# A hybrid backbone step on one core: a third expert fixed ahead of the router, three sets of weight homes, the first expert's rows by selection products

## What is computed

```python
def trunk_layer(P, l, x, cond, ...):
    mod = jnp.dot(jax.nn.silu(cond), P["w_ada"][l]) + P["b_ada"][l]
    sh1, sc1, g1, sh2, sc2, g2 = jnp.split(mod[:, None, :], N_MOD, axis=-1)
    h = rmsnorm(x, P["norm1"][l]) * (1 + sc1) + sh1
    ... four mixers ...
    x = x + g1 * jnp.einsum("blm,md->bld", mixed, P["w_out"][l])
    h = rmsnorm(x, P["norm2"][l]) * (1 + sc2) + sh2
    x = x + g2 * moe_ffn(h, P["w_router"], ...)

def moe_ffn(x, w_router, router_bias, w_gate, w_up, w_down):
    probs = softmax(t @ w_router)           # 384 x 16
    ... best of 4 groups, top 2 inside it, weights normalised ...
    h = silu(t @ w_gate[e]) * (t @ w_up[e]) # 1024 -> 512
    h = h * gates[..., None]
    return sum over e of h @ w_down[e]      # 512 -> 1024
```

## Time and profile before

| | |
|---|---|
| median of 3 runs | 661.88 us |
| profiled execution | 664.11 us, span 662.3 us |
| PE, DVE, ACT, POOL busy in the span | 85%, 37%, 21%, 10% |
| mean granted clock of PE | 0.945 |
| bytes moved | 176.16 MB, 266 GB/s over the span |
| 16 loads each of gate, up and down weights | 2048 KB each |

### The profile page before, as it was taken

The page is one execution under the profiler, slowest core; times in us unless marked ns, Lnnn a source line. Parts: engine busy times, 40 slices in busy tenths (PEclk is TensorE's granted clock), DMA queues, the critical chain, the costliest instruction groups (busy, mean ns, idle before and its releaser), DMA issues.

```text
span 662.3 us, 13154 instructions
## 1 busy us (share of the span) xinstructions
PE 563.9 (85%) x5670; PEld 367.7 (56%) x5670; DVE 246.3 (37%) x526; ACT 137.8 (21%) x260; POOL 66.2 (10%) x98
## 2 busy tenths in 40 slices
PE   2789999999999899599964899999777777867974
PEld 0575544566675566574443799997344444434531
DVE  2551648887736824720358611011000000001025
ACT  1330562422128601010141111000000000000012
POOL 1039000000003100020002000000000000300031
PEclk9989999999999999899977699999999999979988
DMA  8989830303110914961597599999999999999972
GB/s 265 392 300 368 308 128 0 128 1 127 55 74 10 374 72 153 356 176 63 190 406 279 187 353 387 398 384 389 393 396 395 395 396 396 394 365 412 405 273 100
DMA packets 79277, 176.16 MB, mean 266 GB/s; under 512 B 6072, under 2 KB 11199, under 8 KB 78847
## 3 DMA queue, kind: packets, MB, share of 16 engines
q1 hardware_dynamic: 64848, 149.01, 60.6%
q0 software_dynamic: 6032, 18.75, 8.3%
q10 hardware_dynamic: 8351, 7.73, 3.5%
HBM read 163.01 MB, written 12.47 MB: 265 GB/s over the span
## 4 chain that ended last, share of the span: by engine, by line
PE 23%; SPq 19%; DMA 8%; issue 4%; DVE 2%; ACT 1%; POOL 1%; ACTq 0%; DVEq 0%; POOLq 0%
SPq L1091 17%; PE psum L874 6%; PE psum L799 5%; PE psum L871 4%; DMA slot<-in_w_down 3%; PE psum L882 2%; PE psum L806 2%; SPq L1105 2%; DMA y_rows<-ye 1%; DMA h_rows<-ye 1%; DMA slot<-y_rows,rows 1%; DMA xe<-h_rows,lst 1%; PE psum L813 1%; POOL slot L1244 1%; PE psum L459 1%
## 5 line engine op out<-in xcount | busy, mean ns | idle before, releaser
L882 PE MATMUL psum<-slot,xeTa 128*32 128x256 f32 x1536 | 98.9, 415 | 28.8 <-DMA slot<-in_w_gate 25.3
L547 PE MATMUL psum<-hT,slot 128*128 128x384 f32 x304 | 100.8, 489 | 0.0
L882 PEld LDWEIGHTS psum<-slot,xeTa 128*32 128x32 f32 x1536 | 57.4, 119 | 69.7 <-issue 28.8
L547 PEld LDWEIGHTS psum<-hT,slot 128*128 128x128 f32 x304 | 56.9, 190 | 38.2
L882 PE MATMUL psum<-slot,heT 128*32 128x256 f32 x768 | 45.3, 389 | 6.3 <-DMA slot<-in_w_down 6.3
L871 PE MATMUL psum<-slot,xeTa 128*32 128x384 f32 x384 | 44.8, 509 | 0.5 <-ACT xeTa L1542 0.5
L874 PE MATMUL psum<-slot,xeTa 128*32 128x128 f32 x384 | 45.3, 282 | 0.0
L874 PEld LDWEIGHTS psum<-slot,xeTa 128*32 128x32 f32 x384 | 43.4, 114 | 0.6
L556 PE MATMUL psum<-slot,hT 128*128 128x512 f32 x96 | 42.3, 596 | 1.1 <-DMA slot<-in_w_in 1.1
L2214 DVE COPY heT<-psum 128x256 f32<-128x256 f32 (+1 forms) x16 | 7.3, 457 | 95.8 <-PE psum L902 95.8
L1550 ACT ACTIVATE he<-psum 128x256 f32<-128x256 f32 (+1 forms) x16 | 6.6, 410 | 154.9 <-PE psum L882 126.9
(11 more groups left out here) (429 smaller groups left out, 774.8 us busy)
## 6 DMA issues: line engine op xcount, KB each, us to landing
slot<-in_w_gate SPq DMA_DIRECT2D x16, 2048.0 KB, 23.2
slot<-in_w_up SPq DMA_DIRECT2D x16, 2048.0 KB, 18.8
slot<-in_w_down SPq DMA_DIRECT2D x16, 2048.0 KB, 19.7
slot<-in_w_ada SPq DMA_DIRECT2D x12, 2048.0 KB, 15.4
slot<-in_w_in SPq DMA_DIRECT2D x7, 2048.0 KB, 9.0
y_rows<-T POOLq DMA_DIRECT2D x11, 384.0 KB, 15.4
slot<-in_w_out SPq DMA_DIRECT2D x2, 2048.0 KB, 16.3
y_rows<-ye ACTq DMA_DIRECT2D x22, 128.0 KB, 6.8
```

The costliest lines, as they stand in the source:

```text
L547: last = mm(o[:, 0:TOK], w[:, kt, tile(i)], hT[:, kt, :], start=(kt == 0), stop=(kt == KT - 1))
L882: last = mm(psum[32 * c:32 * c + 32, bank, 0:HALF], x(k, c % 2), w(k)[:, c // 2 * HALF:c // 2 * HALF + HALF], start=(k == 0), stop=(k == t ...
```

## The change

1. **A third fixed expert.** `order` puts experts 0, 1 and 2 first. Expert 2's blocks have homes of their own, made of pieces: seven eighths of its gate block lie over constants that only the mixers need, the rest over the new GX, over G1 (the gate of the first residual), hT, badar (the modulation bias) and SELW, which lies over the selection matrices SEL. A load of such a set is 2 + 3 + 5 DMAs. Each piece of expert 2 goes out when what lies there has been used.
2. **Three sets in rotation.** Experts 0 to 11 take the sets n % 3, the last four n % 2. A load waits for the last user of its set, that is n - 3. The loops over ten experts are written out.
3. **Expert 0's rows by products.** DVE writes the 0/1 matrix ONE, PE multiplies it with `h2tok` and gets the rows already turned (24 products, 96 columns each), and ACT copies them to `xeT`. No gather, no turning. `lst2` holds expert 1's list alone and stands between the two halves of these products. The second and third part of the later lists are now made inside the first gate product.
4. **Block 11** of the modulation, on PE, moves from behind `lst2` to before the wait for the router's result. Its sum on DVE (`modrow_out(11)`) moves forward too.
5. **G2** no longer has a tile of its own. It lies over the down home of set 0, and POOL loads it when expert 14's down product is done; G2P is issued behind it.

```diff
-    put("order", np.tile((15 - np.arange(16) + np.array([20000, 10000] + 14 * [0]))[None], (P, 1)))
+    put("order", np.tile((15 - np.arange(16) + np.array([30000, 20000, 10000] + 13 * [0]))[None], (P, 1)))
...
-        G2 = eb("G2", [P, 2, D])
+        GX = eb("GX", [P, 4, CW])
+        G2 = slot[home(0, 2)][:, 0:4, :].rearrange("p (c k) n -> p c (k n)", c=2)
...
+        hTf = hT[:, :, :].rearrange("p k n -> p (k n)")
+        g1f = G1[:, :, :].rearrange("p c n -> p (c n)")
+        spent = cols["dft_ctx"][0]
+        assert cols["mask_b"][0] + P - spent >= (KT - 1) * CW
+        third_gate = [const[:, spent + k * CW:spent + k * CW + CW] for k in range(KT - 1)] + [GX[:, 0, :]]
+        third_up = [GX[:, k, :] for k in range(1, 4)] + [g1f[:, k * CW:k * CW + CW] for k in range(4)] + \
+                   [hTf[:, 2 * CW:3 * CW]]
+        badarf = badar[:, :, :].rearrange("p n g -> p (n g)")
+
+        def of_set(n):
+            return n % 3 if n < 12 else n % 2
+
+        def use(n):
+            return sum(of_set(m) == of_set(n) for m in range(n))
+
+        def user_before(n):
+            return max(m for m in range(n) if of_set(m) == of_set(n))
+        SEL1 = hTf[:, 0:NT * P].rearrange("p (j n) -> p j n", j=NT)
+        ONE = hTf[:, CW:CW + NT * ROWS].rearrange("p (j n) -> p j n", j=NT)
...
+        SELW = eb("SELW", [P, D])
+        third_down = [[hTf[:, 3 * CW:4 * CW], hTf[:, 4 * CW:5 * CW]], [badarf[:, 0:CW], badarf[:, CW:2 * CW]],
+                      [SELW[:, 0:CW], SELW[:, CW:2 * CW]], [hTf[:, 5 * CW:6 * CW], badarf[:, 2 * CW:3 * CW]]]
...
+            ada(11)
             pe.wait_ge(s["route"], 1)
             o = claim(pe, "places")
             for j in range(NT):
...
-            o = claim(pe, "lst2")
+            for j in range(NT):
+                for half in range(2):
+                    taken(pe, ("h2", j, half))
             pe.wait_ge(s["sel"], 1)
-            for e in range(2):
-                for j in range(NT):
-                    last = mm(o[:, e:e + 1], SEL[:, 2 * j + e, :], tokid16[:, j:j + 1], start=(e == 0 and j == 0),
-                              stop=(j == NT - 1), skip_group_check=True)
-            fill(last, "lst2")
-            ada(11)
+            for half in range(2):
+                o = claim(pe, ("first", half))
+                for kt in range(KT // 2):
+                    c = kt * ROWS
+                    for j in range(NT):
+                        last = mm(o[:, c:c + ROWS], h2tok[j][:, tile(half * 4 + kt)], ONE[:, j, :], start=(j == 0),
+                                  stop=(j == NT - 1), skip_group_check=True)
+                fill(last, ("first", half))
+                if half == 0:
+                    o = claim(pe, "lst2")
+                    pe.wait_ge(s["sel"], 2)
+                    for j in range(NT):
+                        last = mm(o[:, 0:1], SEL1[:, j, :], C("tokid")[:, j:j + 1], start=(j == 0), stop=(j == NT - 1))
+                    fill(last, "lst2")
...
-            def packed(bank, x, w, terms):
+            def packed(bank, x, w, terms, between=()):
 
                 for k in range(terms):
+                    if k in between:
+                        later_lists(between.index(k) + 1)
...
+            def weights(n, k):
+
+                if of_set(n) == 2:
+                    name, count = (("third_gate", 32), ("third_up", 48), ("third_down", 80))[k]
+                    pe.wait_ge(s[name], count * (use(n) + 1))
+                    return (third_gate, third_up, third_down)[k]
+                p = of_set(n)
+                pe.wait_ge(loaded[home(p, k)], 16 * (use(n) + 1 + (PRE_USES if p else 0)))
+                return halves_of(slot[home(p, k)]) if k == 2 else rows_of(slot[home(p, k)])
+                up(n % 2, 2, weights(n, 0), n, (3, 6) if n == 0 else ()).then_inc(s["gate_done"], 1)
...
-            load_x(0, 0, 0)
-            later_lists(1)
-            gate(0, 0, 0)
-            later_lists(2)
-            load_x(1, 1, 0)
-            experts(0, True, False)
-            experts(1, False, False)
-            with pe.Fori(2, E // 2 - 1) as it:
-                experts(it, False, False)
-            pe.wait_ge(s["sel"], NT + 2)
+            for half in range(2):
+                taken(pe, ("first", half))
+            gate(0)
+            load_x(1)
+            for n in range(E - 2):
+                expert(n)
...
+            def third_gate_a(e):
+                sp.dma_start(pieces(const[:, spent:spent + (KT - 1) * CW], 0, KT - 1), source(e, 0)[:, 0:KT - 1, :]
+                             ).then_inc(s["third_gate"], 16)
+
+            def third_gate_b(e):
+                sp.dma_start(GX[:, 0:1, :], source(e, 0)[:, KT - 1:KT, :]).then_inc(s["third_gate"], 16)
...
+            def third_down_a(e):
+                sp.dma_start(hTf[:, 3 * CW:5 * CW], source(e, 2)[:, 0, :]).then_inc(s["third_down"], 16)
+                sp.dma_start(hTf[:, 5 * CW:6 * CW], source(e, 2)[:, 3, 0:CW]).then_inc(s["third_down"], 16)
...
+            sp.wait_ge(s["hy_done"], 1)
+            sp.wait_ge(s["rope"], 1)
+            taken(sp, ("rsl", 3))
+            third_gate_a(2)
             take(sp, ("rm", 1))
             sp.wait_ge(s["state_out"], 16 * 3)
             for k in range(3):
                 load_expert(0, 0, k, 0)
             load_pre(len(PRE) - 1)
-            for k in range(3):
+            for k in range(2):
                 key = PRE[len(PRE) - NS + k]
                 take(sp, last_of[key[0]](key[1]))
                 load_expert(1, 1, k, 0)
+            third_gate_b(2)
+            third_up_a(2)
+            sp.wait_ge(s["x1"], NT)
+            third_up_b(2)
+            taken(sp, ("h2", NT - 1, 1))
+            third_up_c(2)
+            key = PRE[-1]
+            take(sp, last_of[key[0]](key[1]))
+            load_expert(1, 1, 2, 0)
+            third_down_a(2)
+            taken(sp, ("ada", 11))
+            third_down_b(2)
+            sp.wait_ge(s["sel_used"], NT)
+            third_down_c(2)
+
+            def reload(n, k):
+
+                e = sp.value_load(perm[0:1, n:n + 1], min_val=0, max_val=E - 1)
+                sp.wait_ge(s[("gate_done", "up_done", "down_done")[k]], user_before(n) + 1)
+                if of_set(n) < 2:
+                    load_expert(e, of_set(n), k, 0)
+                elif k == 0:
+                    third_gate_a(e)
+                    third_gate_b(e)
...
 
             sp.wait_ge(s["perm"], 1)
-            reload(2, 0, 0, 1)
-            with sp.Fori(1, E // 2 - 1) as it:
-                for p in range(2):
-                    n = 2 * it + p
-                    reload(n, p, 1, it)
-                    reload(n + 1, 1 - p, 0, it + p)
-                    reload(n, p, 2, it)
...
+            reload(3, 0)
+            for n in range(3, E):
+                reload(n, 1)
+                if n + 1 < E:
+                    reload(n + 1, 0)
+                reload(n, 2)
...
-            for n in range(E):
-                if n == 0:
+            for n in range(1, E):
+                if n == 1:
                     taken(pool, "lst2")
+                    taken(pool, ("first", 1))
                 elif n == 2:
                     pool.wait_ge(s["lists"], 1)
-                if n >= 2:
-                    pool.wait_ge(s["xt_filled"], n - 1)
+                if n >= 3:
+                    pool.wait_ge(s["xt_filled"], n - 2)
...
+            pool.wait_ge(s["down_done"], E - 1)
             pool.dma_start(G2[:, :, :], A["gate_rows"][1:2].to_broadcast([P, 2, D])).then_inc(s["g2_in"], 16)
...
-            xt_out(0, 0, False)
+            for half in range(2):
+                o = take(act, ("first", half))
+                give(a(xeTa[:, 0, half * 4:half * 4 + 4, :].rearrange("p k n -> p (k n)"), o[:, 0:4 * ROWS], ACT.Copy
+                       ), ("first", half))
...
-            v.tensor_tensor(SEL[:, 0:2 * NT, :].rearrange("p (j e) n -> p j e n", e=2),
-                            C("count")[:, 0:P].unsqueeze(1).unsqueeze(1).to_broadcast([P, NT, 2, P]),
-                            R[10][:, :, 0:2].unsqueeze(3).to_broadcast([P, NT, 2, P]), ALU.is_equal).then_inc(s["sel"], 1)
-            o = take(dve, "lst2")
-            give(v.tensor_copy(lst[:, 0:2], o[:, 0:2]), "lst2")
+            taken(dve, ("h2", NT - 1, 1))
+            v.tensor_tensor(ONE, C("count")[:, 0:ROWS].unsqueeze(1).to_broadcast([P, NT, ROWS]),
+                            R[10][:, :, 0:1].to_broadcast([P, NT, ROWS]), ALU.is_equal).then_inc(s["sel"], 1)
+            v.tensor_tensor(SEL1, C("count")[:, 0:P].unsqueeze(1).to_broadcast([P, NT, P]),
+                            R[10][:, :, 1:2].to_broadcast([P, NT, P]), ALU.is_equal).then_inc(s["sel"], 1)
+            modrow_out(11)
...
-            modrow_out(11)
```

184 lines of the change are left out of this document (102 added, 82 removed).

## The result

655.29 us (median of 654.47, 656.00, 654.58 and 657.02) against 662.84 for the kernel before in the same session. The ratio on record is 0.9896, 95% interval 0.9867 to 0.9925, that is 6.9 us less (the two medians alone are 7.6 apart). One of the five executions behind that median was a slow one, 849.65 us at a mean clock of 0.651, and the ratio leaves it out. The prediction said 17.0 less, 645, and its range ended at 654. The profiled execution took 654.47 us, with a span of 652.6, 9.7 less than the one of before.

What follows compares the result with a forecast made beforehand. DMA bytes over bandwidth bound it from about 470 us, PE and DMA both nearly full from 379 to 470. -15.9 - 2.7 + 1.1 + 0.5 = -17.0 from 661.88 gave 645 us; forecast 642 to 649, wider range 640 to 654.

Steps and rivals of the forecast that it cites:

- Part 2: Expert 0's rows: 24 products take 7.2 us, first gate product at 365.7; PE gains 3.5 us, not added to the sum.
- Part 1: Third fixed expert: 4.07 MB net fill DMA's hole from 358 to 379; 15.9 us fewer loads, start 2.7 us earlier.
- Part 3: Block 11 fits into the 4.36 us router wait at no cost; expert 1's down weights issue at about 353.
- Part 4: Three-set rotation: DMA is asked 2 to 3 us before it is free; 21 pieces at 0.05 us cost 1.1 us.
- Part 5: The end, with G2 loaded late: 0.5 us of loss, between -0.6 and +4.
- Rival (b): Smaller gain: stretch after the hole loses 3.1 us more, G2P holds up the gathers by 4; 652 us, chance 0.16.
- (a): Larger gain: pieces cost nothing, DMA moves 395 instead of 378 GB/s after the hole; 640 us, chance 0.13.
- (c): Third set changes nothing since PE always frees the home; only PE's 3.5 us remain, 658.4 us, chance 0.05.
- (d): Slower: pieces charged one by one in the full stretch, 1.6 us each, 34 us; 678 us, chance 0.05.
- (e): Third set's pieces come late, PE waits once for 2 us; 647 us, counted within the forecast's chance of 0.58.

Runs made afterwards that it cites:

- c4_short: Changed kernel with 8 instead of 24 products for the first expert's rows, and the second and third later lists behind the first gate product; 648.3 us.
- d1_warm: Changed kernel with 18 idle products on PE, nine in the router's wait and nine in the wait for the first selection matrix; 649.01 us.
- a1_same: Changed kernel timed again without an edit in a later session; 653.64 us, ratio 0.9853 against the kernel before.
- a4_rot6: Changed kernel with the third set used for two experts instead of four; 9.5 us less than the kernel before.
- b2_pieces: Kernel before with each expert load cut into four DMAs, 144 DMAs more; 2.2 us more than the kernel before.
- b5_unroll: Kernel before with the loops over pairs of experts written out on all engines; 2.8 us more than the kernel before.
- c1_g2late: Kernel before with the loads of G2 and G2P held back until expert 14's down product is done; 0.4 us less than the kernel before.
- f1_warm_before: Kernel before with block 11 moved into the router's wait and idle products in PE's waits up to the first gate product; 6.0 us more.
- e5_ada_before: Kernel before with only modulation block 11 moved into the router's wait; 2.2 us more than the kernel before.
- e1_pe_unroll: Kernel before with only PE's loop over pairs of experts written out; median 666.10 us, 3.6 us more than the kernel before.
- a2_g2: Changed kernel with G2 loaded earlier, into the spent constants' space; median 657.02 us, 6.0 us less than the kernel before.
- c2_nog2: Changed kernel with the loads of G2 and G2P left out; 14.4 us less than the kernel before.
- d2_g2pe: Changed kernel with G2 made on chip by PE instead of loaded; median 653.72 us, 11.1 us less than the kernel before.
- d3_both: Changed kernel with 18 idle products on PE and G2 made by PE; 648.90 us, 14.2 us less than the kernel before.

## Why the prediction was wrong

The sign was right, and so was the mechanism of parts 1, 3 and 4 (a hole in DMA's stream, filled by a third expert that is fixed ahead of the router). Two steps of the sum were not, and together they make some 8 of its 17 us: PE's products ahead of the first sorted load, priced too low and then given no weight, and the written-out loops, which the sum does not have.

**Part 2 is the step that failed.** "I take the upper one at half clock, as it is a product and not a turn: 7.2 us." The half clock was right, the duration was not. At a granted clock of 0.5 a product with a 128 by 128 operand in fp32 took 0.43 us with 96 columns and 0.40 with a single one (the three of lst2, 364.46 to 365.66). So the group of four side by side, at 0.40, was the nearer row and needed no factor of 96/128. The 24 took 9.7 us and not 7.2, 2.5 more, although the clock rose before the last of them. lst2 stands inside, 1.2 us that the sum 358 + 7.2 + 0.5 leaves out. They started 1.3 us later than 358, which is the lateness of this execution and no fault of the step, and 0.3 came behind them. So the first gate product came at 370.94 and not at 365.7. I then wrote that PE's gain "is not added to the sum, because DMA is busy until 376.3 anyway". That was the overlap that failed: DMA is busy until then only with what is already issued, and the next load needs the first gate home. It went out at 378.98, and 368 to 379 moved 292 GB/s. The text prices that at 1.4 us; c4_short and d1_warm show 4.6 and 4.9, because the window behind is thinner too (330 GB/s from 379 to 400, where d1_warm has 376). The two windows together, 11 x 0.075 + 21 x 0.046 = 1.8 MB, are 4.5 us at 0.395 MB/us. They compare two executions of which one was 4.0 us behind, so that they agree so well is in part luck; with a1_same's 236 and 349 GB/s it would be 5.1.

**The written-out loops were not in the sum at all.** I took the change for the moves that its title names. That PE, ACT, DVE and SP lose their loops over pairs of experts stands in the diff; in the kernel before it costs 2.8 to 3.6 us.

**Part 1** held in its size: from 358 to 379 DMA moved 4.1 MB more than before, where 4.07 were forecast (3.5 in a1_same), though the last piece (0.5 MB) went out only at 377.32. **Part 3** held, and carries more than I said: without it everything else is worth nothing. The down weights of expert 1 went out at 358.16 and not at 353, behind the pieces in SP's queue, which cost nothing, as DMA moved 408 GB/s from 358 to 368.

**Part 4**: 0.05 us a piece was three times too much; at 0.015 the 21 cost 0.3 us. The fixed 2.0 us a DMA that the prediction takes from the Trainium skill, page "DMA: Bandwidth & Descriptors", section "Anatomy of one DMA", is fitted there to DMAs issued by GpSimd, while the pieces stand in SP's queue. That the full stretch would run at 395 was wrong: from 450 to 550 all twelve profiles of the changed kernel and its variants have 381 to 386, and all seven of the kernel before and its variants 392 to 395. That is 2 us in this window. a4_rot6 speaks against the rotation, b2_pieces against the pieces (393 GB/s), b5_unroll against the loops (392); part of it may be that PE handles more experts in that window (1379 product records for 1248), with their small writes, but no run shows it. It stays open.

**Part 5**: 0.5 us net agrees with c1_g2late, -0.4 [-2.1, +1.3], in the kernel before. In the changed kernel's first profile the tail is 2.5 us longer, in a1_same 0.9 (30.1 for 29.1). The last down product, forecast at about 615.5, started at 620.97, because the stream was late.

**The sum again:** -17.0 + 4.6 (hole) + 3.2 (loops) - 0.8 (pieces) = -10.0; with the open 2 us, -8.0. Measured -9.8 and -6.9. That prices from different kernels and sessions add up is assumed; no run undoes both at once. The profiles alone divide it otherwise: the span fell by 9.7 us where 17.0 were forecast, and of the 7.3 between, 4.0 lie ahead of the first sorted load (1.3 later for 2.7 sooner, 1.5 of it this execution's lateness), 1.3 between that load and the last down product (242.0 us for 255.5, with 14.8 fewer forecast), and 2.0 in the tail. In a1_same they are 1.8, 3.4 and 0.4.

Rival (b), 652, had nearly the size, but by other causes. The gathers did begin 4 us late in the first profile, but what POOL waited for was expert 14's write and not G2P; and the stretch from 379 to 450 lost 8 GB/s of 378 there, which is 1.5 us, but only 1 GB/s in a1_same. (a), (c) and (d) are out: 0.015 us a piece is far from (d)'s 0.86. Of (e) nothing was seen; PE's first wait for weights comes at some 493 us.

## What to carry to other kernels

Where DMA's stream must start the moment PE frees a buffer, the work on PE just ahead of that is on the path even if both look busy around it: moving that start by 5.6 to 7.3 us moved the end by six to nine tenths of it, in three kernels (c4_short and d1_warm against a1_same, f1_warm_before against e5_ada_before). Price it from the row whose operands have the same shape, and look at the granted clock there. If PE stands idle ahead of it, 18 idle products gave 4.9 us here (3.2 in the pair of one session), but they must stand ahead of a wait and not behind one: 28 behind one made the start 5.6 us later. Before two profiles are compared by position, look for a row ahead of the change and see how far apart they are there; here it was up to 4 us. Of a diff that also turns loops into straight code, price the code; and when a load is moved, look at what is queued behind it.

## What the runs showed of the hardware

- An fp32 product with a 128 by 128 stationary operand and 96 moving columns took 0.43 us at a granted clock of 0.5 and 0.22 at 1.0 (d1_warm); with one moving column it took 0.40 at 0.5.
- The clock fell to 0.5 at 359, after windows of 3 us in which PE was busy 0.89 and 0.38 us; with idle products in the same places it stayed at 1.00 until the first gate product was done (d1_warm).
- DMAs of 0.5 MB in one queue instead of 2 MB cost 0.015 us each in a full stream (b2_pieces).
- PE's loop over pairs of experts written out cost 3.6 us of 663 [2.0, 5.2], with 0.18 MB more of code fetched (e1_pe_unroll).
- From the issue of expert 14's write (two DMAs of 128 KB) to the gather that waited for it, 11.2 and 12.7 us passed with 1.57 MB of G2 and G2P issued beside it (the changed kernel, a1_same), and 3.2 to 7.7 in the five profiles without (before, a2_g2, c2_nog2, d2_g2pe, d3_both).
